# Expert weights of a routed FFN in one 8 MB and two 2 MB transfers instead of eight smaller ones

## The chip, the core and the metric

The kernel runs on one core of a Trainium2 chip. A core has TensorE (PE; its weight loads are PEld), VectorE (DVE), ScalarE (ACT), GpSimd (POOL) and SyncE (SP), which issues almost all transfers here, and 16 DMA engines that move the bytes. The metric is the device time of one execution in microseconds, as a median of runs. MB in this text is 2^20 bytes, except in the GB/s and MB columns of the profile.

## What is computed

A decoder layer on 256 tokens of width 1024: RMSNorm, a combined projection, three token mixers (attention, short convolution, cross-attention), a gated merge and an output projection, and after it a mixture of 32 experts of which each token takes four. In fp32, an expert's up matrix is 1024 x 2048 (8 MB) and its down matrix 1024 x 1024 (4 MB):

```python
def expert_block(args):
    xb, e = args
    gu = xb @ w_gu[e] + b_gu[e]
    g = jnp.minimum(gu[:, :D_EXPERT], SWIGLU_LIMIT)
    lin = jnp.clip(gu[:, D_EXPERT:], -SWIGLU_LIMIT, SWIGLU_LIMIT)
    glu = g * jax.nn.sigmoid(SWIGLU_ALPHA * g)
    return ((lin + 1.0) * glu) @ w_down[e] + b_down[e]
```

Each token's four results are weighted and added to the residual stream, and a last RMSNorm follows. All 32 experts are used, so 384 MB of expert weights have to come out of HBM whatever the routing.

## The kernel before

Raw instruction streams, one per engine, tied together by semaphores. The first 300 us compute the mixers; the rest is a loop over the 32 experts, each with 64 token slots (a second pass over the experts would run only if an expert drew more than 64 tokens).

**Buffers.** `ring` has 16 slots of 8 KB per partition. Up matrices go in as 8 slots each: even experts in slots 8 to 15, odd experts in 0 to 7, so two ups fit. `dring` has four such slots and holds one down matrix. PE counts what it has used up: `pieces_used` goes up by one for each of an expert's eight up slots, `downs_used` by one for each of its four down slots.

**Transfers.** SP issues them all in one order and waits before each for the slots that it overwrites. `expert_up` issues four transfers of 2 MB (`up_pair`: 256 rows of the matrix, two neighbouring rows and so a run of 16 KB for each partition). `expert_down` issues four of 1 MB (`down_piece`: 256 rows, two rows and so 8 KB for each partition). Each lands on its own semaphore (`piece_in`, `down_in`), and PE waits for each just before the matmuls that read it. Which row lies on which partition doesn't matter to the sum, as long as the moving operand is permuted alike: ACT writes `h2` and DVE writes the hidden product in that permuted order.

**Order on SP.** Experts 0 and 1's ups and expert 0's down are loaded while the mixers still run. After that comes the main loop: up(2), down(1), up(3), down(2), and so on up to up(23), down(22): a down comes one expert behind the ups. Then down(23), and the last eight experts in order: up(24), down(24), ..., up(31), down(31). I call the second part the in-order stretch and the place between them, where down(22) and down(23) follow each other directly, the switch. `b_down` and the last norm's gain come behind down(31).

**Order on PE.** For each expert: up matmuls (L1256, 64 recorded matmuls), then what lies between (transposes, the gather of the next tokens, the scatter of the expert before; ACT and DVE make the hidden product), then down matmuls (L1292, 32), and on to the next expert. Expert by expert, in order.

Of the kernel before, what the change touches and what calls it, by code (L numbers as in the profile page):

```python
# [18 lines left out]
P = 128  # L19
# [6 lines left out]
E = 32  # L26
# [88 lines left out]
def build(nc, a, out, scratch, ctx):  # L115
# [110 lines left out]
    in_pairs = "p (j q c) -> p j c q"  # L226
    hid_pairs = hid.rearrange(in_pairs, j=2, c=2)
    sg_pairs = sg.rearrange(in_pairs, j=2, c=2)
    hid_even_odd = g_sb.rearrange("p (j c q) -> p j c q", j=2, c=2)
# [8 lines left out]
    g_pairs = region_r[:, 6140:6148]  # L238
# [16 lines left out]
    def sem(name):  # L255
        return ctx.enter_context(nc.semaphore(name))
# [6 lines left out]
    final_gain_in, out_done, g_pairs_in = sem("final_gain_in"), sem("out_done"), sem("g_pairs_in")  # L263
# [38 lines left out]
    def _(sp):  # L302
# [34 lines left out]
        def up_pair(expert, slot, m):  # L337
            sp.dma_start(ring[:, slot:slot + 2, :].rearrange("p k n -> p (k n)"),  # L338
                         a["w_gu"][0, bass.ds(expert, 1), m * 256:(m + 1) * 256, :]
                         .rearrange("e (p k) n -> p (e k n)", k=2)).then_inc(piece_in[slot], 16)  # L340

        def expert_up(expert, slot0, uses):
# [5 lines left out]
        def down_piece(expert, j):  # L348
            sp.dma_start(dring[:, j, :], a["w_down"][0, bass.ds(expert, 1), j * 256:(j + 1) * 256, :]
                         .rearrange("e (p c) n -> p (e c n)", c=2)).then_inc(down_in[j], 16)  # L350

        def expert_down(expert, uses):
# [7 lines left out]
        for n in range(MIX_RING):  # L360
            used = N_MIX - MIX_RING + 1 + n
            sp.wait_ge(pieces_used, used)
            if n < MIX_RING - 8 and n % 2:
                up_pair(0, 8 + n - 1, n // 2)
            elif n % 2:
                up_pair(1, n - (MIX_RING - 8) - 1, (n - (MIX_RING - 8)) // 2)
            if used == N_PROJ + 12:
                down_piece(0, 2)
            if used == N_PROJ + 17:
                down_piece(0, 0)  # L370
                down_piece(0, 1)
            if used == N_MIX - 1:
                up_pair(0, 14, 3)
            if used == N_MIX:
                up_pair(0, 12, 2)
        down_piece(0, 3)
# [27 lines left out]
    def _(pool):  # L404
# [14 lines left out]
        pool.dma_start(g_pairs.rearrange("p (m k) -> p m k", k=2),  # L419
                       bass.AP(a["rows"].tensor, 16 * P, [[2, P], [256, 4], [1, 2]])).then_inc(g_pairs_in, 16)  # L420
# [3 lines left out]
    def _(act):  # L424
# [180 lines left out]
    def _(dve):  # L605
# [288 lines left out]
        def gathered_half(ps, n, half):  # L894

            dve.tensor_tensor(xg[n][:, 4 * half:4 * half + 4, :], ps[:, :].rearrange("p (c s) -> p c s", c=4),  # L896
                              g_pairs[:, 4 * half:4 * half + 4].unsqueeze(2).broadcast_to([P, 4, 2 * SLOTS]), ALU.mult)\
                .then_inc(xg_sb, 1)
# [35 lines left out]
        dve.wait_ge(g_pairs_in, 16)  # L934
# [8 lines left out]
        with dve.Fori(0, more * (E // 4) + E // 4) as i:  # L943
            for u in range(4):
# [12 lines left out]
                dve.tensor_tensor(hid_even_odd, hid_pairs, sg_pairs, ALU.mult).then_inc(hid_ready, 1)  # L957
# [32 lines left out]
    def _(pe):  # L990
# [251 lines left out]
        with pe.Fori(0, more * (E // 4) + E // 4) as i:  # L1242
            for u in range(4):
                s = i * 4 + u
                slot0 = 8 if u % 2 == 0 else 0

                pe.wait_ge(up_read, s + 1)
# [38 lines left out]
                for c in range(KC):  # L1286
                    if c % 2 == 0:
                        pe.wait_ge(down_in[c // 2], (s + 1) * 16)
                    lhsT = hidT[:, (c % 4) * P + 64 * (c // 4):(c % 4) * P + 64 * (c // 4) + 64]
# [4 lines left out]
                    if c % 2:  # L1294
                        last.then_inc(downs_used, 1)

# [44 lines left out]
```

## Time and profile before

| | |
|---|---|
| median of 3 runs | 1223.33 us (1222.9 to 1224.2) |
| span of the profiled execution | 1221.0 us |
| PE busy | 1116.0 us (91%) |
| DVE, ACT busy | 387.3 us (32%), 263.7 us (22%) |
| moved by DMA | 452.06 MB, mean 370 GB/s |

The span is that of one profiled execution; it is 2.3 us short of the median, which has what lies around it. The page cuts the span into 40 slices of 30.5 us. Landing is when a transfer's semaphore reaches its full count, and is read from SP's issue rows.

### The profile page before, as it was taken

How to read it: one execution, taken by the hardware profiler on the slowest of the kernel's cores; microseconds unless marked ns; L12 is line 12 of the kernel's file. 1: busy time of each engine (PE TensorE's matmuls, PEld its weight loads, DVE VectorE, ACT ScalarE, POOL GpSimd, SP SyncE). 2: the span in 40 equal slices, each digit the busy share in tenths (PEclk: the TensorE clock that was granted, in tenths of full speed). 3: DMA queues.
4: the chain of work that ended last, by engine and by line, in shares of the span. 5: the costliest groups of instructions: out<-in, count | busy, mean ns of one | idle time of the engine just before them, and what ended most of it. 6: DMA issues, size and time to landing. Idle time of an engine off the chain costs nothing.

```text
span 1221.0 us, 15367 instructions
## 1 busy us (share of the span) xinstructions
PE 1116.0 (91%) x6083; PEld 581.7 (48%) x6083; DVE 387.3 (32%) x716; ACT 263.7 (22%) x403; POOL 9.0 (1%) x11
## 2 busy tenths in 40 slices
PE   5999999998999988888888898898888899988886
PEld 4999999995343333333333333333333333333332
DVE  6657655574122212212121212122222222221213
ACT  5334475443011111111111111111111111111112
POOL 2000000000000000000000000000000000000000
PEclk8999999999999999999999999999999999999998
DMA  7984354667999999999999999999999999999994
GB/s 263 346 271 158 120 165 161 235 234 309 428 425 425 426 428 426 426 427 427 426 427 426 427 426 426 427 427 426 425 426 425 428 426 425 428 426 425 428 424 189
DMA packets 74642, 452.06 MB, mean 370 GB/s; under 512 B 5058, under 2 KB 36023, under 8 KB 41847
## 3 DMA queue, kind: packets, MB, share of 16 engines
q1 hardware_dynamic: 74055, 449.94, 90.3%
q0 software_dynamic: 560, 1.74, 0.5%
q8 instruction: 20, 0.33, 0.1%
q14 instruction: 7, 0.06, 0.0%
HBM read 450.60 MB, written 1.06 MB: 370 GB/s over the span
## 4 chain that ended last, share of the span: by engine, by line
DMA 50%; PE 43%; DVE 4%; SPq 1%; issue 1%; ACT 0%; DVEq 0%; ACTq 0%
DMA dring<-in_w_down_dram 40%; PE bank L1001 19%; PE bank L1256 10%; DMA ring<-in_w_gu_dram 9%; PE bank L1292 9%; SPq L338 1%; DVE region_r L954 1%; DVE region_r L957 1%; DVE region_r L950 1%; PE bank L1276 1%; DVE region_r L951 1%; PE bank L1226 1%; PE bank L1178 1%; DVE memT_low L645 0%; PE bank L1065 0%
## 5 line engine op out<-in xcount | busy, mean ns | idle before, releaser
L1256 PE MATMUL bank<-ring,region_x 128*64 128x512 f32 x2048 | 449.6, 595 | 14.4 <-DMA ring<-in_w_gu_dram 14.4
L1292 PE MATMUL bank<-dring,region_r 128*64 128x512 f32 x1024 | 241.2, 608 | 55.3 <-DMA dring<-in_w_down_dram 54.4
L1256 PEld LDWEIGHTS bank<-ring,region_x 128*64 128x64 f32 x2048 | 143.0, 137 | 300.6 <-issue 273.6
L1292 PEld LDWEIGHTS bank<-dring,region_r 128*64 128x64 f32 x1024 | 67.9, 138 | 214.4 <-DMA dring<-in_w_down_dram 109.1
L950 DVE TENSOR_SCALAR region_r<-bank 128x512 f32<-128x512 f32 x32 | 22.1, 692 | 371.3 <-PE bank L1256 371.3
L968 DVE SCALAR_TENSOR_TENSOR y_parts<-bank,region_r,y_parts 64x512 fp32r<-64x512 f32 x32 | 23.8, 744 | 338.1 <-ACT y_parts L589 338.1
L580 ACT ACTIVATE region_r<-region_r 128x512 f32<-128x512 f32 x32 | 20.1, 629 | 436.3 <-DVE region_r L950 436.3
L1001 PE MATMUL bank<-hT_high,w_high 128*128 128x256 f32 x384 | 111.0, 289 | 0.0
L1001 PE MATMUL bank<-hT_low,w_high 128*128 128x256 f32 x384 | 108.8, 283 | 0.0
L1001 PE MATMUL bank<-hT_high,w_low 128*128 128x256 f32 x384 | 108.8, 283 | 0.0
L655 DVE TENSOR_TENSOR w_low<-ring,w_high 128x2048 fp32r<-128x2048 f32 x39 | 89.2, 2290 | 55.4 <-ACT w_high L443 55.1
L443 ACT ACTIVATE w_high<-ring 128x2048 fp32r<-128x2048 f32 x40 | 76.4, 1911 | 73.2 <-PE bank L1001 71.2
L588 ACT ACTIVATE y_parts<-bank,region_r 64x512 fp32r<-64x512 f32 x32 | 21.8, 682 | 300.1 <-PE bank L1292 300.1
L1001 PEld LDWEIGHTS bank<-hT_high,w_high 128*128 128x128 f32 x384 | 73.7, 192 | 2.0 <-issue 1.7
L1001 PEld LDWEIGHTS bank<-hT_low,w_high 128*128 128x128 f32 x384 | 73.7, 192 | 0.5 <-issue 0.5
L1001 PEld LDWEIGHTS bank<-hT_high,w_low 128*128 128x128 f32 x384 | 73.7, 192 | 0.0
L1220 PE MATMUL bank<-region_r,region_h 128*128 128x128 f32 x544 | 66.2, 276 | 1.4 <-DVE region_r L890 1.4
L1220 PEld LDWEIGHTS bank<-region_r,region_h 128*128 128x128 f32 x544 | 63.4, 192 | 1.5 <-issue 1.5
L1178 PE MATMUL bank<-y_parts,scaT 128*128 128x512 f32 x132 | 47.6, 444 | 0.0
L585 ACT ACTIVATE region_r<-bank 128x512 f32<-128x512 f32 x32 | 19.1, 598 | 55.0 <-PE bank L1276 55.0
L1226 PE MATMUL bank<-b_parts,sel 128*128 128x512 f32 x65 | 29.2, 449 | 1.3 <-DVE region_x L896 0.7
L1276 PE MATMUL bank<-consts,region_r 128*128 128x128 f32 x128 | 21.0, 287 | 9.6 <-DVE region_r L957 9.6
(230 smaller groups left out, 909.1 us busy)
## 6 DMA issues: line engine op xcount, KB each, us to landing
ring<-in_w_gu_dram SPq DMA_DIRECT2D x128, 2048.0 KB, 29.6
dring<-in_w_down_dram SPq DMA_DIRECT2D x128, 1024.0 KB, 27.2
ring<-in_w_in_dram SPq DMA_DIRECT2D x26, 1024.0 KB, 9.6
ring<-in_w_mem_kv_dram SPq DMA_DIRECT2D x4, 1024.0 KB, 11.7
ring<-in_w_out_dram SPq DMA_DIRECT2D x4, 1024.0 KB, 4.8
ring<-in_w_br_conv_dram SPq DMA_DIRECT2D x2, 1024.0 KB, 5.0
ring<-in_w_br_att_dram SPq DMA_DIRECT2D x2, 1024.0 KB, 6.1
ring<-in_w_br_xatt_dram SPq DMA_DIRECT2D x2, 1024.0 KB, 5.2
```

What stands on the lines that cost most here:

```text
L443: act.activation(w_high[p % 3][:, :], ring[:, q, :], ACT.Copy).then_inc(w_high_ready, 1)
L588: act.activation(y_parts[0:64, 0:512], y_ps[0:64, :], ACT.Copy, scale=w_slot[0:64, :])
L655: dve.tensor_tensor(w_low[q][:, :], ring[:, q, :], w_high[p % 3][:, :].bitcast(fp32), ALU.subtract)\
L950: dve.tensor_scalar(g_sb, gate_ps[:, :], LIMIT, None, ALU.min).then_inc(g_ready, 1)
L968: dve.scalar_tensor_tensor(y_parts[64:128, 0:512], y_ps[0:64, :], w_slot[0:64, :], y_parts[0:64, 0:512].bitcast(fp32), ALU.mult, ALU.subtract)
L1001: ins = mm(dst, lhsT[l][at_l], rhs[r][at_r], start=first and n == 0, stop=last and n == 2)
L1178: last = mm(acc[t][half][:, :], scaT[n][:, t, :], y_parts[:, half * 512:half * 512 + 512], start=False, stop=stop)
L1220: last = mm(ps[:, c * P:(c + 1) * P], h2[:, t, at:at + P], gat[:, t, :], start=(t == 0), stop=(t == TT - 1))
L1226: mm((gate_ps, lin_ps)[k][:, :], sel[:, :], b_parts[:, k * 512:k * 512 + 512], start=True, stop=False)
L1256: last = mm(ps[64 * half:64 * half + 64, :], xg[u // 2][:, c, 64 * (u % 2):64 * (u % 2) + 64], ring[:, slot0 + c, k * F + half * 512:k * F ...
L1276: last = transpose(gate_ps[:, c * P:(c + 1) * P], g_sb[:, c * P:(c + 1) * P], ident)
L1292: last = mm(y_ps[64 * half:64 * half + 64, :], lhsT, dring[:, c // 2, at:at + 512], start=(c == 0), stop=(c == KC - 1))
```

## The change

The up matrix of an expert is loaded by one transfer of 8 MB: partition p gets rows 8p to 8p+7, one run of 64 KB. The down matrix comes in two transfers of 2 MB, four rows of each half for a partition, one run of 16 KB. So SP waits for all eight up slots to be free before it issues an up, and for two down slots before each half of a down; PE waits for a whole up before its first up matmul, and for half a down. The bytes, the buffers and the order of matrices on SP stay as they were.

At the edges the transfers keep their former sizes: experts 0 and 1's ups, expert 0's down, up(2) (four of 2 MB) and up(31) (four of 2 MB) and down(31) (four of 1 MB). There a run is cut from the 64 KB (or 16 KB) row group, so it is again 16 KB (8 KB) long. PE's loop over four experts becomes a function, called in the loop for experts 0 to 27 and once more, written out, for 28 to 31, because only there it waits for the smaller transfers again. The permutations on ACT and DVE follow the new row order.

```diff
+        def up_chunks(expert, slot, c, n):
+            sp.dma_start(ring[:, slot:slot + n, :].rearrange("p k n -> p (k n)"),
+                         a["w_gu"][0, bass.ds(expert, 1), :, :]
+                         .rearrange("e (p k) n -> p (e k n)", k=KC)[:, c * PIECE:(c + n) * PIECE]).then_inc(piece_in[slot], 16)
-            for m in range(KC // 2):
-                sp.wait_ge(pieces_used, uses + 2 * m + 1)
-                up_pair(expert, slot0 + 2 * m, m)
+        def expert_up(expert, slot0, uses, n=KC):
+            for c in range(0, KC, n):
+                sp.wait_ge(pieces_used, uses + c + n - 1)
+                up_chunks(expert, slot0 + c, c, n)
-            for j in range(DRING):
-                sp.wait_ge(downs_used, uses + j)
-                down_piece(expert, j)
+        def expert_down(expert, uses, n=2):
+            for j in range(0, DRING, n):
+                sp.wait_ge(downs_used, uses + j + n - 1)
+                down_slots(expert, j, n)
...
+        expert_up(2, 8, N_MIX - RING + 17, 2)
+        expert_down(1, 1)
+        expert_up(3, 0, N_MIX - RING + 25)
+        expert_down(2, 5)
-        with sp.Fori(0, more * (E // 2) + (E // 2 - 1 - IN_ORDER)) as i:
+        with sp.Fori(1, more * (E // 2) + (E // 2 - 1 - IN_ORDER)) as i:
...
-        with sp.Fori(0, IN_ORDER) as i:
+        with sp.Fori(0, IN_ORDER - 1) as i:
...
+        expert_up(E - 2, 8, ups + (E - 2) * KC)
+        expert_down(E - 2, downs + (E - 2) * DRING)
+        expert_up(E - 1, 0, ups + (E - 1) * KC, 2)
+        expert_down(E - 1, downs + (E - 1) * DRING, 1)
...
-            act.activation(h2[:, t, :].rearrange("p (m k q) -> p m k q", m=4, k=2),
-                           x2[:, t, :].rearrange("p (m q k) -> p m k q", m=4, k=2),
+            act.activation(h2[:, t, :].rearrange("p (k q) -> p k q", k=8),
+                           x2[:, t, :].rearrange("p (q k) -> p k q", k=8),
...
-                dve.tensor_tensor(hid_even_odd, hid_pairs, sg_pairs, ALU.mult).then_inc(hid_ready, 1)
+                dve.tensor_tensor(hid_by_row, hid_fours, sg_eights, ALU.mult).then_inc(hid_ready, 1)
...
-                    if c % 2 == 0:
+                    if c == 0:
                         pe.wait_ge(piece_in[slot0 + c], i * 32 + 16 * (u // 2) + 16 * (loads_before(slot0 + c) + 1))
+                    elif c % 2 == 0 and (u < 3 or last_one):
+                        pe.wait_ge(piece_in[slot0 + c], 16 * (loads_before(slot0 + c) + 1 + u // 2))
...
-                    if c % 2 == 0:
+                    if c % 4 == 0:
                         pe.wait_ge(down_in[c // 2], (s + 1) * 16)
+                    elif c % 2 == 0:
+                        pe.wait_ge(down_in[c // 2], 32 if last_one else 16)
```

On SP at the start of the expert loop: `ring` transfers are ups, `dring` transfers downs, 128x4096 is 16 KB for each partition. Before, one half of the loop body, which loads one up and one down:

```order
L338 ISA [waits pieces_used]
L338 DMA ring<-in_w_gu_dram 128x4096
L345 REGISTER_ALU
L338 ISA [waits pieces_used]
L338 DMA ring<-in_w_gu_dram 128x4096
L345 REGISTER_ALU
L338 ISA [waits pieces_used]
L338 DMA ring<-in_w_gu_dram 128x4096
L345 REGISTER_ALU
L338 ISA [waits pieces_used]
L338 DMA ring<-in_w_gu_dram 128x4096
```

Now, what stands ahead of the loop, for up(2), down(1), up(3) and down(2):

```order
L339 DMA ring<-in_w_gu_dram 128x4096 [waits pieces_used] x4
L352 DMA dring<-in_w_down_dram 128x4096 [waits downs_used] x2
L339 DMA ring<-in_w_gu_dram 128x16384 [waits pieces_used]
L352 DMA dring<-in_w_down_dram 128x4096 [waits downs_used] x2
```

Up(3) is the first that has one wait, for the last of its eight slots, in the place of four.

On SP at the switch, down(23) behind down(22). Before:

```order
L349 DMA dring<-in_w_down_dram 128x2048 [waits downs_used]
L355 REGISTER_ALU
L349 DMA dring<-in_w_down_dram 128x2048 [waits downs_used]
L355 REGISTER_ALU
L349 DMA dring<-in_w_down_dram 128x2048 [waits downs_used]
L355 REGISTER_ALU
L349 DMA dring<-in_w_down_dram 128x2048 [waits downs_used]
L388 UNCONDITIONAL_BRANCH
```

Now:

```order
L352 DMA dring<-in_w_down_dram 128x4096 [waits downs_used]
L359 REGISTER_ALU
L352 DMA dring<-in_w_down_dram 128x4096 [waits downs_used]
L396 UNCONDITIONAL_BRANCH
```

The first half of down(23) waits until PE has used two slots of down(22), where its first quarter waited for one.

## Rows read from the trace of the kernel before

**Rows 1.** The page: DMA share and rate in 40 slices, packets, chain by engine.

```profile
DMA  7984354667999999999999999999999999999994
GB/s 263 346 271 158 120 165 161 235 234 309 428 425 425 426 428 426 426 427 427 426 427 426 427 426 426 427 427 426 425 426 425 428 426 425 428 426 425 428 424 189
DMA packets 74642, 452.06 MB, mean 370 GB/s; under 512 B 5058, under 2 KB 36023, under 8 KB 41847
DMA 50%; PE 43%; DVE 4%; SPq 1%; issue 1%; ACT 0%; DVEq 0%; ACTq 0%
```

**Rows 2.** Waits in total: engine, line, what for; us, times, longest.

```profile
PE bank L1292 <- DMA dring<-in_w_down_dram: 54.4, 68, 1.6
```

**Rows 3.** Timeline of PE: start, length; down(s) as its quarters land, 600-660 us.

```profile
624.00 1.94 PE L1292 MATMUL bank<-dring,region_r 128*64 128x512 f32 x8 [1.53 <-DMA dring<-in_w_down_dram]
...
631.46 1.94 PE L1292 MATMUL bank<-dring,region_r 128*64 128x512 f32 x8 [0.55 <-DMA dring<-in_w_down_dram]
```

**Rows 4.** The same, the last up and what follows, 1180-1211 us.

```profile
1182.44 3.65 PE L1256 MATMUL bank<-ring,region_x 128*64 128x512 f32 x16 [0.62 <-DMA ring<-in_w_gu_dram]
...
1192.22 3.65 PE L1256 MATMUL bank<-ring,region_x 128*64 128x512 f32 x16 [1.24 <-DMA ring<-in_w_gu_dram]
...
1200.22 7.09 PE L1292 MATMUL bank<-dring,region_r 128*64 128x512 f32 x32
1207.23 3.70 PE L1300 MATMUL bank<-ring,region_r 32*128 32x512 f32 x8
```

**Rows 5.** Windows: stretch, engines' busy us, PEclk, DMA share, GB/s; mixer weights load.

```profile
40.00:45.00 5.00, 5.00 (x44) 5.00 (x43) 2.98 (x2) 1.92 (x1) 0.00 (x0) 1.00 1.10 348
```

**Rows 6.** Timeline of SP: the four issues of up(3).

```profile
328.25 10.58 SPq L338 DMA_DIRECT2D ring<-in_w_gu_dram  x4
```

**Rows 7.** One issue by line: the first of up(2), with its time to landing.

```profile
L338 SPq DMA_DIRECT2D ring<-in_w_gu_dram x1: 346/346/346, 302.6 to 302.6; - x1
...
DMA to landing us min/median/max: 7.7/7.7/7.7
```

**Rows 8.** The same, the last of up(3).

```profile
L338 SPq DMA_DIRECT2D ring<-in_w_gu_dram x1: 332/332/332, 338.5 to 338.5; - x1
...
DMA to landing us min/median/max: 17.1/17.1/17.1
```

**Rows 9.** Timeline of PE: up(1), down(1), up(2), 320-352 us.

```profile
324.38 13.96 PE L1256 MATMUL bank<-ring,region_x 128*64 128x512 f32 x64
...
342.68 7.09 PE L1292 MATMUL bank<-dring,region_r 128*64 128x512 f32 x32
...
350.12 13.96 PE L1256 MATMUL bank<-ring,region_x 128*64 128x512 f32 x64
```

**Rows 10.** Timelines at the switch: PE at down(22), SP at down(23).

```profile
948.68 1.94 PE L1292 MATMUL bank<-dring,region_r 128*64 128x512 f32 x8 [1.54 <-DMA dring<-in_w_down_dram]
...
956.12 1.94 PE L1292 MATMUL bank<-dring,region_r 128*64 128x512 f32 x8 [0.54 <-DMA dring<-in_w_down_dram]
...
950.66 7.77 SPq L349 DMA_DIRECT2D dring<-in_w_down_dram  x4
```

**Rows 11.** Windows and PE's timeline at 800 us; then the window at 15 us.

```profile
800.00:805.00 5.00, 3.92 (x12) 1.12 (x14) 0.00 (x0) 0.00 (x0) 0.00 (x0) 0.66 1.02 423
...
801.08 7.07 PE L1292 MATMUL bank<-dring,region_r 128*64 128x512 f32 x24 [1.51 <-DMA dring<-in_w_down_dram]
...
15.00:20.00 5.00, 0.38 (x1) 0.38 (x2) 4.67 (x6) 2.03 (x6) 2.84 (x2) 0.63 1.10 348
```

**Rows 12.** The page, section 6: a 1 MB transfer with runs of 4 KB.

```profile
ring<-in_w_out_dram SPq DMA_DIRECT2D x4, 1024.0 KB, 4.8
```

**Rows 13.** By line: DVE's contiguous product, its permuted one, ACT's h2; min/median/max ns.

```profile
L954 DVE SCALAR_TENSOR_TENSOR region_r<-region_r x32: 691/693/694, 314.0 to 1197.3; 128x512 f32<-128x512 f32 x32
...
L957 DVE TENSOR_TENSOR region_r<-region_r x32: 691/691/695, 314.8 to 1198.0; 128x512 f32<-128x512 f32 x32
...
L568 ACT ACTIVATE region_h<-region_x,norm 128x1024 f32<-128x1024 f32 x2 | 2.3, 1202 | 0.0
```

More of the change, by code:

```diff
@@ L225, in build @@
     hidT = region_r[:, 3072:3584]
[L226 to L229, printed above, removed]
+    in_fours = "p (q k) -> p k q"
+    hid_fours = hid.rearrange(in_fours, k=4)
+    sg_eights = sg.rearrange(in_fours, k=4)
+    hid_by_row = g_sb.rearrange("p (k q) -> p k q", k=4)
     x2T = region_r[:, 0:2048].rearrange("p (c t) -> p c t", c=KC)
@@ L335, in _, with down_slots @@
         sp.dma_start(x_again, a["x"][0].rearrange("(t p) d -> p t d", p=P)).then_inc(x_again_in, 16)
[L337 to L342, printed above, removed]
-            for m in range(KC // 2):
-                sp.wait_ge(pieces_used, uses + 2 * m + 1)
-                up_pair(expert, slot0 + 2 * m, m)
[L348 to L352, printed above, removed]
-            for j in range(DRING):
-                sp.wait_ge(downs_used, uses + j)
-                down_piece(expert, j)
+        def up_chunks(expert, slot, c, n):
[6 more added lines that the diff above has]
+                up_chunks(expert, slot0 + c, c, n)
+        def down_slots(expert, j, n):
+            m, k = j // 2, j % 2
+            sp.dma_start(dring[:, j:j + n, :].rearrange("p k n -> p (k n)"),
+                         a["w_down"][0, bass.ds(expert, 1), m * 512:(m + 1) * 512, :]
+                         .rearrange("e (p k) n -> p (e k n)", k=4)[:, k * PIECE:(k + n) * PIECE]).then_inc(down_in[j], 16)
+        def expert_down(expert, uses, n=2):
+            for j in range(0, DRING, n):
+                sp.wait_ge(downs_used, uses + j + n - 1)
+                down_slots(expert, j, n)
         for n in range(MIX_RING):
@@ L363, in _ @@
             if n < MIX_RING - 8 and n % 2:
-                up_pair(0, 8 + n - 1, n // 2)
+                up_chunks(0, 8 + n - 1, n - 1, 2)
             elif n % 2:
-                up_pair(1, n - (MIX_RING - 8) - 1, (n - (MIX_RING - 8)) // 2)
+                up_chunks(1, n - (MIX_RING - 8) - 1, n - (MIX_RING - 8) - 1, 2)
             if used == N_PROJ + 12:
-                down_piece(0, 2)
+                down_slots(0, 2, 1)
             if used == N_PROJ + 17:
-                down_piece(0, 0)
-                down_piece(0, 1)
+                down_slots(0, 0, 1)
+                down_slots(0, 1, 1)
             if used == N_MIX - 1:
-                up_pair(0, 14, 3)
+                up_chunks(0, 14, 6, 2)
             if used == N_MIX:
-                up_pair(0, 12, 2)
-        down_piece(0, 3)
+                up_chunks(0, 12, 4, 2)
+        down_slots(0, 3, 1)
         sp.wait_ge(passes_ready, 1)
         more = sp.value_load(more_i32[0:1, 0:1], min_val=0, max_val=PASSES - 1)
-        with sp.Fori(0, more * (E // 2) + (E // 2 - 1 - IN_ORDER)) as i:
+        expert_up(2, 8, N_MIX - RING + 17, 2)
[3 more added lines that the diff above has]
+        with sp.Fori(1, more * (E // 2) + (E // 2 - 1 - IN_ORDER)) as i:
             expert_up((i * 2 + 2) % E, 8, i * 16 + (N_MIX - RING + 17))
@@ L418, in _ @@
         pool.dma_start(b_rt, a["b_router"].broadcast_to([P, E])).then_inc(router_in, 16)
-        pool.dma_start(g_pairs.rearrange("p (m k) -> p m k", k=2),
-                       bass.AP(a["rows"].tensor, 16 * P, [[2, P], [256, 4], [1, 2]])).then_inc(g_pairs_in, 16)
+        pool.dma_start(g_eights, bass.AP(a["rows"].tensor, 16 * P, [[8, P], [1, 8]])).then_inc(g_eights_in, 16)
     @block.scalar
@@ L896, in gathered_half @@
             dve.tensor_tensor(xg[n][:, 4 * half:4 * half + 4, :], ps[:, :].rearrange("p (c s) -> p c s", c=4),
-                              g_pairs[:, 4 * half:4 * half + 4].unsqueeze(2).broadcast_to([P, 4, 2 * SLOTS]), ALU.mult)\
+                              g_eights[:, 4 * half:4 * half + 4].unsqueeze(2).broadcast_to([P, 4, 2 * SLOTS]), ALU.mult)\
                 .then_inc(xg_sb, 1)
@@ L933, in _ @@
         bias_selector(0)
-        dve.wait_ge(g_pairs_in, 16)
+        dve.wait_ge(g_eights_in, 16)
         dve.wait_ge(gathered, 1)
@@ L1241, in _, with four_experts @@
         more = pe.value_load(more_i32[0:1, 0:1], min_val=0, max_val=PASSES - 1)
-        with pe.Fori(0, more * (E // 4) + E // 4) as i:
+        def four_experts(i, last_four):
             for u in range(4):
@@ L1245, in _ @@
                 slot0 = 8 if u % 2 == 0 else 0
+                last_one = last_four and u == 3
                 pe.wait_ge(up_read, s + 1)
@@ L1295, in _ @@
                         last.then_inc(downs_used, 1)
+        with pe.Fori(0, more * (E // 4) + (E // 4 - 1)) as i:
+            four_experts(i, False)
+        four_experts(more * (E // 4) + (E // 4 - 1), True)
         pe.wait_ge(b_down_in, 16)
```

4 lines of the change are left out of this document (2 added, 2 removed).

## The prediction

> **What bounds the kernel now.** I read the page's slices first. From slice 11 to slice 39, some 880 of 1221 us, the DMA engines are busy all the time and move 424 to 428 GB/s [rows 1]; the chain puts half of the span on DMA. Then the waits: PE stands 54 us in total ahead of its down matmuls until a quarter of a down lands, in 68 waits of at most 1.6 us [rows 2]. An expert takes PE 25.74 us from the start of one up to the start of the next when nothing is late (350.12 - 324.38) [rows 9]. The transfers take longer. Quarters of a down land 2.487 us apart (7.46/3) [rows 3], quarters of an up 4.89 us (9.78/2) [rows 4], so an expert takes the engines 4 x 4.89 + 4 x 2.487 = 29.5 us. From about 305 to 1201 us the time is thus set by bytes, and only a faster stream, or a hole in it, moves the end; behind the last transfer PE counts.
>
> **What a transfer costs beyond its bytes.** Let x be the time of a MB and y what eight runs add on an engine (128 partitions on 16 engines). The page counts 32,795 packets of 8 KB or more [rows 1]; 128 ups of four and 128 downs' quarters with 128 runs each give 2 x 16,384 = 32,768, so a run is a packet. x + y = 2.487 and 2x + y = 4.89 give y = 0.084. A third point: the mixers' weights come in runs of 1 KB, 64 for each engine and MB, at 348 GB/s [rows 5], 3.01 us for a MB: x + 8y = 3.01, and with the first equation y = 0.075, x = 2.41. I take 0.075, since its lever is longer. It is a cost of the packet (9 ns), as eight times more packets in one transfer cost eight times more.
>
> The Trainium skill (DMA: Bandwidth & Descriptors, "Why small descriptors are slow") names about 3 cycles for each packet inside the engine; at the 850 MHz of its specifications that would be an estimated 28 ns for eight, and the saving below 4 us where I get 10.8. The rows show over twice that, and the measurement decides.
>
> **Saved in the stream.** Ups 3 to 30 go from four transfers to one, and 32 runs on an engine to 8: 28 x 3 = 84 times y. Downs 1 to 30 go from four to two: 30 x 2 = 60. Together 144 x 0.075 = **10.8 us** (7 to 13 by the spread of y). That the 64 KB run is still one packet isn't in the trace; see the rivals. An expert then takes 8x + y + 2(2x + y) = 19.36 + 9.79 = 29.15 us.
>
> **Added at the start.** Up(3) was issued in four parts from 328.25 on [rows 6], the last at 338.5, and that one landed at 355.6 [rows 8]. Now the whole waits for what the last part waited for, PE's end of up(1) [rows 9], so it is issued at 338.5. What was issued before it, up to down(1), would be through by 335. So the queue runs empty. Into an empty queue a 2 MB transfer landed 7.7 us after its issue [rows 7], 2.8 more than its 4.9 in the stream. Up(3) lands at 338.5 + 2.8 + 19.36 = 360.7, 5.1 later than before, though 5y = 0.4 of the saving lie ahead of that point: the hole costs **5.5 us**. From up(4) on PE frees an up well ahead. In the main loop, with L the landing of a down's second half: PE needs 3.5 for that half, 0.4 to the next up and 14 for it, so the next up is issued at about L + 18.3 and wanted at L + 29, less 2.8. That is covered.
>
> **Added at the switch.** Down(22) and down(23) follow each other in one ring. Before, PE began a quarter at 948.68 and SP refilled it at 950.66 [rows 10], 2.0 later, while 7.4 us of quarters were still in the queue. Now, with X the landing of down(22)'s second half, PE begins the first at X - 4.9 and needs 3.5 + 0.2; the refill is issued at X - 1.1 and lands at X - 1.1 + 2.8 + 4.9 = X + 6.6 where the stream would have X + 4.9: **1.7 us**. It is nothing if the 2.8 are hidden, 3.4 if PE's clock is low there.
>
> **In the in-order stretch** PE starts an up when all of it has landed, at U. It reaches down at U + 18.3 (342.68 - 324.38), frees its first half at U + 22.1, and down(e+1) may be issued from there; it is wanted at U + 29.15 less 2.8, so 4.3 us are left. PE then waits 29.15 - 25.74 = 3.4 us for each up in one piece. Before, it worked on an up while that came in, in waits of 0.62 and 1.24 us [rows 4].
>
> **Added at the end.** Before, PE started the last quarter of up(31) on its landing at 1192.22 and was done with down(31) at 1207.23, 15.0 later [rows 4]. Now PE starts up(30) at U, up(31) at U + 25.7, down(31) at U + 44.0 and is done at U + 51.05, as it can't catch up: all of up(31) is there by U + 9.79 + 4 x 4.895 = U + 29.4. That is 21.7 behind the last up's landing where it was 15.0, **6.7 us** more. Smaller pieces for expert 31 alone don't help, since PE is still busy with expert 30.
>
> **The clock.** After 1.51 us of waiting ahead of down the granted clock was 0.66 in the window 800 to 805 us, between the levels of 1.2 and 2.4 GHz, and 24 matmuls took 7.07 us [rows 11], where 32 take 7.09: 7.07 - 5.32 = 1.75 us lost. In the window 15 to 20 us, in which PE was busy for only 0.38 us, it was 0.63. The new waits of 3.4 us are over twice as long as the 1.51, so I take a fall at every up of the in-order stretch. Six of them are covered (27.5 < 29.15), that of up(30) isn't: **1.7 us** (0 to 1.7).
>
> The Trainium skill (TensorE: Matmul & The Clock Gate, "HAM oscillation") says that waiting for a transfer ahead of each group of matmuls makes each group start slow. By it the 1.7 are due; without it the sum is 1.7 less.
>
> **Nothing, or bounded.** DVE's permuted product (step 2) takes 691 ns, the contiguous one 693 [rows 13], so a step of 4 should cost nothing; were it doubled, 0.7 us an expert would disappear in PE's waits, save one or two at the end. ACT's h2 reads with step 8 where it was 2, 1.2 us each [rows 13]: 0, at most 2.3 once. The runs of the edge transfers are as long as before. PE's written-out last four experts might have to be fetched behind long packets; the slack of the in-order stretch covers a few us.
>
> A longer run may land later: runs of 4 KB landed 4.8 us after issue [rows 12], about 2.2 more than their 2.6 in the stream, runs of 16 KB 2.8 more. Drawn on in proportion to 64 KB this adds 2.4 once at the start and once at the end. I take 0, being nearest to the row of 16 KB, and keep 4.8 for the range.
>
> **Sum** against the profiled span of 1221.0: -10.8 + 5.5 + 1.7 + 6.7 + 1.7 = +4.8, so 1225.8; with the 2.3 us between span and median, 1228.1. The three edges eat the saving and more.
>
> **Rivals.**
> 1. *Edges cheaper, within 0.2%.* No fall of the clock at up(30), and the refill at the switch hidden: +1.4, 1224.7. For it: behind the wait of 1.54 us at 948.68 [rows 10] the eight matmuls took 1.94 us, as they do at full clock.
> 2. *Faster.* Long runs also raise the rate of bytes. About 350 MB are in the new transfers; each 1% off x = 2.41 is worth 8.4 us, so 1219.7 at 1%. It decides from 0.9% on, where 7.2 us more are saved and the sum passes -2.4. Against it: runs of 1, 8 and 16 KB fit one x, so nothing points to a better one. The Trainium skill (DMA: Bandwidth & Descriptors, "Specifications") gives the port side a ceiling of 435 GB/s, which is this x; by it the rival can't be.
> 3. *The 64 KB run is cut*, into four of 16 KB as before: the ups' 84y = 6.3 are lost, +11.1, 1234.4. The trace has no run over 16 KB.
> 4. *Long runs disturb each other in HBM.* Runs of neighbouring partitions start 64 KB apart where it was 16, so what is read at once lies four times further apart. At 1% it costs 8.4 us: 1236.5. No row here speaks for or against it. The Trainium skill (DMA: Bandwidth & Descriptors, "Latency and other measured facts") tells of row pitches of 2 MB and more that cut the rate and one of 512 KB that didn't; 64 KB is below them.
> 5. *Late landing of long runs*, above: +9.6, 1232.9.
>
> **Chances.** Forecast 0.47; rival 1 0.22; 2 0.13; 3 0.08; 4 0.05; 5 0.05. A measurement of this kernel can tell about 0.2% (2.4 us) from no change, so: faster 0.13, same 0.22, slower 0.65. The range 1221 to 1236 leaves out the better half of rival 2 and the worse of 4.
>
> **What would show it.** In the trace after: a DMA slice near 340 us with a hole of 5 us; landings of an expert 29.15 us apart (29.5: rival 3; under 29.0: rival 2; over 29.6: rival 4); packets near 74,600 - 84 x 128 - 60 x 128 = 56,200 (67,000 if cut); PE waits of 3.4 us ahead of ups in the last 230 us with a clock under 1.00 behind them; PE's end of down(31) 21.7 to 23.4 us behind the last up's landing. Without the hole or the longer end the forecast is wrong.

## The result, and the profile after

The changed kernel takes **1235.7 us** (median of 4 runs, 1231.1 to 1236.8) where the kernel before takes 1223.7 beside it: 1.009 times as long, 95% interval 1.0077 to 1.0102, so 0.9% slower. The forecast was 1228.1 us with a range of 1221 to 1236: the direction is right, the time lies 0.3 us inside the upper edge of the range, and the loss is 12 us where I had 4.8. The profiled execution is the shortest of the four, with a span of 1229.1 us, 8.1 over that of before.

The page after: share and rate in 40 slices, packets, chain. To be read beside [rows 1].

```profile
DMA  7984344667899999999999999999999999999992
GB/s 260 344 274 162 120 168 146 240 252 303 374 387 439 433 444 420 433 444 416 437 444 414 439 444 414 427 430 433 431 431 432 394 429 417 429 432 430 431 424 93
DMA packets 53910, 452.13 MB, mean 368 GB/s; under 512 B 2754, under 2 KB 33719, under 8 KB 39543
DMA 50%; PE 44%; DVE 3%; ACT 1%; issue 1%; SPq 0%; DVEq 0%; ACTq 0%
```

The stream is faster in the middle (432 GB/s on average from 500 to 900 us, where it was 426), and three places are worse: slices 11 and 12 (374 and 387), slice 32 (394), and the last, which holds almost no transfers any more (93 where it was 189). There are 14,367 packets of 8 KB or more; 32,795 - 84 x 128 - 60 x 128 = 14,363 were due if a run of 64 KB is one packet. So rival 3 is out by the row of packets. 2,304 packets under 512 B are gone too. That is 144 transfers fewer times 16 engines, so each transfer brings a small packet on each engine; experiment 2, with three transfers more, has 49 more of them.

**The start.** Windows (engines' busy us, PEclk, DMA share, GB/s), then the one issue of up(3) with its landing, in the changed kernel:

```profile
335.00:337.00 2.00, 2.00 (x12) 0.72 (x10) 0.00 (x0) 0.00 (x0) 0.00 (x0) 1.00 0.02 8
337.00:339.00 2.00, 2.00 (x13) 0.58 (x8) 0.00 (x0) 0.00 (x0) 0.00 (x0) 1.00 0.00 0
...
L339 SPq DMA_DIRECT2D ring<-in_w_gu_dram x1: 328/328/328, 339.6 to 339.6; - x1
...
DMA to landing us min/median/max: 23.2/23.2/23.2
```

Here is the hole: 4 us in which nothing moves, while PE is busy. Up(3) is issued at 339.6 and lands at 362.8, where its last part landed at 355.6 [rows 8].

**The main loop and the switch.** PE's timeline at down(22), and SP's issues of down(23) and up(24):

```profile
950.61 3.65 PE L1309 MATMUL bank<-dring,region_r 128*64 128x512 f32 x16 [1.63 <-DMA dring<-in_w_down_dram]
955.48 3.65 PE L1309 MATMUL bank<-dring,region_r 128*64 128x512 f32 x16 [1.21 <-DMA dring<-in_w_down_dram]
...
988.22 15.65 PE L1271 MATMUL bank<-ring,region_x 128*64 128x512 f32 x64 [2.53 <-DMA ring<-in_w_gu_dram]
...
954.31 5.20 SPq L352 DMA_DIRECT2D dring<-in_w_down_dram  x2
960.06 0.35 SPq L339 DMA_DIRECT2D ring<-in_w_gu_dram  x1
```

Each matmul group that waits starts on a landing. From down(22)'s second half to the whole of up(24) it takes 988.22 - 955.48 = 32.7 us; a down and an up in the stream are 29.15. The bubble, a stretch in which the queue has too little to do, is 3.6 us. It comes in two equal parts: the refill issued at 954.31 lands at 962.15, 6.7 us behind down(22), and the one issued at 959.17 lands at 968.83, 6.7 us behind the first, where 4.9 were due each time.

**The end.** PE's timeline from up(30) on. Compare [rows 4]:

```profile
1134.87 15.65 PE L1271 MATMUL bank<-ring,region_x 128*64 128x512 f32 x64 [2.04 <-DMA ring<-in_w_gu_dram]
...
1164.03 13.95 PE L1271 MATMUL bank<-ring,region_x 128*64 128x512 f32 x64 [1.27 <-DMA ring<-in_w_gu_dram]
...
1182.70 7.09 PE L1309 MATMUL bank<-dring,region_r 128*64 128x512 f32 x32
1190.14 13.95 PE L1271 MATMUL bank<-ring,region_x 128*64 128x512 f32 x64
...
1208.82 7.09 PE L1309 MATMUL bank<-dring,region_r 128*64 128x512 f32 x32
1215.84 3.70 PE L1321 MATMUL bank<-ring,region_r 32*128 32x512 f32 x8
```

From up(30)'s landing on PE never waits for a transfer again; up(31) starts 26.1 us later, though three of its four parts had landed. The last part lands at 1193.4, PE is done with down(31) 22.4 us after that, where it took 15.0.

**Two costs that I had put at nothing.** By line: DVE's product and PE's wait for it, ACT's h2 and PE's gather behind it.

```profile
L968 DVE TENSOR_TENSOR region_r<-region_r x32: 1057/1069/1082, 315.6 to 1206.3; 128x512 f32<-128x512 f32 x32
...
  PE bank L1291: 21.7, 32
...
289.06 4.17 ACT L579 ACTIVATE region_h<-region_x,norm 128x1024 f32<-128x1024 f32 x2
...
293.28 3.84 PE L1231 MATMUL bank<-region_r,region_h 128*128 128x128 f32 x32 [2.07 <-ACT region_h L579]
```

DVE's product takes 1069 ns with a step of 4 elements where it took 691 with a step of 2 [rows 13], and PE waits 0.68 us for it in each expert where it waited 0.30. ACT's two h2 instructions take 4.17 us together where they took 2.31, and PE now stands 2.07 us before the gather and begins it 0.85 us later.

Where the 8.1 us of this execution are, by the same events in both traces (positive: later than before):

| event | before | after | step |
|---|---|---|---|
| PE starts up(1) | 324.38 | 325.62 | +1.2: h2, product |
| up(3) has landed | 355.6 | 362.8 | +6.0: hole |
| down(22) has landed | 956.1 | 955.5 | -7.8: 102 times eight packets less |
| down(23) has landed | 966.0 | 968.9 | +3.5: switch |
| up(31) has landed | 1192.2 | 1193.4 | -1.7: 35 times eight packets less (2.7), 1.0 lost again, 0.8 of it at up(29) |
| PE is done with down(31) | 1207.2 | 1215.8 | +7.4: end |

That is +8.6, and what follows is 0.5 shorter. Up to down(22) the 102 are 20 ups (4 to 23) at 3 and 21 downs (2 to 22) at 2, so eight packets cost 7.8/102 = 0.076 us, which I had read as 0.075. The two steps at the hole and the switch are net of such savings, 0.4 and 0.15.

### The profile page after: what moved, and what is told of

Read it like the earlier page. It is cut to its first block, busy times and chain, and to the rows that moved or that the text cites. A ratio compares the mean times of both kernels' runs of the same rounds, so it can differ in the third digit from the quotient of the medians.

```text
span 1229.1 us, 14723 instructions
## 1 busy us (share of the span) xinstructions
PE 1117.4 (91%) x6083; PEld 588.3 (48%) x6083; DVE 399.1 (32%) x716; ACT 266.1 (22%) x403; POOL 8.8 (1%) x11
## 4 chain that ended last, share of the span: by engine, by line
DMA 50%; PE 44%; DVE 3%; ACT 1%; issue 1%; SPq 0%; DVEq 0%; ACTq 0%
DMA dring<-in_w_down_dram 40%; PE bank L1012 19%; PE bank L1309 11%; DMA ring<-in_w_gu_dram 10%; PE bank L1271 9%; DVE region_r L968 1%; PE bank L1019 0%; DVE region_r L965 0%; DVE region_r L961 0%; DMA consts<-in_consts_dram 0%; DVE memT_low L656 0%; PE bank L1076 0%; PE bank L1291 0%; PE bank L1056 0%; DVE region_r L962 0%
## 5 line engine op out<-in xcount | busy, mean ns | idle before, releaser
L1271 PEld LDWEIGHTS bank<-ring,region_x 128*64 128x64 f32 x2048 | 145.7, 138 | 302.1 <-issue 285.5
L1309 PEld LDWEIGHTS bank<-dring,region_r 128*64 128x64 f32 x1024 | 72.4, 141 | 201.5 <-issue 129.1
L1231 PEld LDWEIGHTS bank<-region_r,region_h 128*128 128x128 f32 x544 | 63.3, 192 | 2.2 <-ACT region_h L579 2.2
L968 DVE TENSOR_TENSOR region_r<-region_r 128x512 f32<-128x512 f32 x32 | 34.2, 1069 | 1.1
L596 ACT ACTIVATE region_r<-bank 128x512 f32<-128x512 f32 x32 | 19.2, 599 | 66.9 <-PE bank L1291 66.9
```

Source lines behind the costliest of these rows:

```text
L968: dve.tensor_tensor(hid_by_row, hid_fours, sg_eights, ALU.mult).then_inc(hid_ready, 1)
L1231: last = mm(ps[:, c * P:(c + 1) * P], h2[:, t, at:at + P], gat[:, t, :], start=(t == 0), stop=(t == TT - 1))
L1271: last = mm(ps[64 * half:64 * half + 64, :], xg[u // 2][:, c, 64 * (u % 2):64 * (u % 2) + 64], ring[:, slot0 + c, k * F + half * 512:k * F ...
L1309: last = mm(y_ps[64 * half:64 * half + 64, :], lhsT, dring[:, c // 2, at:at + 512], start=(c == 0), stop=(c == KC - 1))
```

## Experiments

Times are medians; "changed" is the changed kernel. All are beside runs of the kernel before on the same chip (1223.8 to 1224.2 us).

**1. The changed kernel again**, for what its longer executions have more.

> The changed kernel once more, for a second trace of it: its four executions so far lay between 1231.1 and 1236.8 us and the trace in hand is that of the shortest. My account of that trace against before (span 1229.1 against 1221.0): -10.4 us in the stream, +1.2 from a longer h2 on ACT, +6.0 hole at up(3), +3.6 at the switch, +7.4 at the end, +1 of scatter. I expect this trace to show the same terms within 1 us, plus what the longer executions have more, 3 to 5 us: either a fall of TensorE's clock at up(30) (1.7 us, up matmuls 15.65 instead of 13.95 us), or, if the rival is right that long runs make the 16 engines run apart, landings late by several us somewhere in the stream with a longer hole behind them.

Measured: 1233.7 us (1231.8 to 1235.8), the trace's span 1233.8, 4.7 over the first trace. The stream is the same: ups are issued 29.14 us apart ((917.63 - 480.56)/15) as in the first ((915.42 - 478.36)/15). The difference stands in two rows of PE, each with its window:

```profile
294.13 5.47 PE L1231 MATMUL bank<-region_r,region_h 128*128 128x128 f32 x32 [2.07 <-ACT region_h L579]
...
294.00:299.00 5.00, 4.87 (x29) 4.87 (x30) 3.12 (x18) 0.07 (x1) 0.00 (x0) 0.66 0.75 320
...
1165.73 16.87 PE L1271 MATMUL bank<-ring,region_x 128*64 128x512 f32 x64 [2.95 <-DMA ring<-in_w_gu_dram]
...
1165.00:1172.00 7.00, 6.26 (x16) 1.86 (x18) 1.13 (x5) 0.07 (x1) 0.00 (x0) 0.53 0.99 421
```

Behind the wait for h2 the granted clock is 0.66 and the gather takes 5.47 us where it took 3.84: 1.6. Behind the wait for up(30) it is 0.53, nearly all of those 7 us at the lower level of 1.2 GHz, and the up takes 16.87 us where it takes 13.95: 2.9, with nothing behind it to cover them. The first trace had neither fall. Of the start's 2.5 us (1.6, and 0.9 of a mixer stage that ended later) 1.7 are left when up(30) lands (1165.73 against 1164.03), and 1.7 + 2.9 is the 4.7. So between these two traces the difference is for the most part TensorE's clock behind new waits, and the engines running apart were not needed to explain it.

All the traces taken together show how far this goes. Eight of them have the wait of 2.07 us for h2: five then take 5.3 to 5.5 us for the gather and three take 3.84. Seven load up(30) whole: it takes 13.95 us in the first trace alone, 15.65 in three, and 16.87 to 16.96 in three. The first trace is the exception, and its wait there was the shortest (1.27). Up(30) in experiments 2 and 4:

```profile
1162.86 15.65 PE L1271 MATMUL bank<-ring,region_x 128*64 128x512 f32 x64 [2.94 <-DMA ring<-in_w_gu_dram]
...
1163.39 16.96 PE L1271 MATMUL bank<-ring,region_x 128*64 128x512 f32 x64 [3.13 <-DMA ring<-in_w_gu_dram]
```

**2. Up(3) in four transfers.**

```diff
-        expert_up(3, 0, N_MIX - RING + 25)
+        expert_up(3, 0, N_MIX - RING + 25, 2)
```

> Up(3) in four transfers of 2 MB again, all else as in the changed kernel. Theory (the queue runs empty because up(3) waits for all eight slots): landing of up(3)'s last part 6 us earlier, no hole near 340 us, time 5.5 to 6 us under the changed kernel. Rival (the hole is made good later, since PE is the bound in the first experts and waits there anyway): within 1 us of the changed kernel.

Measured: 1231.3 us (1229.5 to 1233.7), 2.4 under the first experiment, with ranges that overlap, so neither. The landing of up(3) did come 7.1 us earlier, counted from expert 0's start (341.7 + 16.1 - 301.6 = 56.2, where changed has 63.3). But the next up has the hole. Its window and issue:

```profile
362.00:370.00 8.00, 8.00 (x47) 3.98 (x44) 2.03 (x4) 1.11 (x3) 0.00 (x0) 1.00 0.82 315
...
L339 SPq DMA_DIRECT2D ring<-in_w_gu_dram x1: 352/352/352, 368.0 to 368.0; - x1
...
DMA to landing us min/median/max: 23.2/23.2/23.2
```

Again 23.2 us from issue to landing, the time of a whole up into an empty queue. Down(2) was through at 357.8 + 9.8 = 367.6, and up(4) would have landed at 387.0; it landed at 391.2, 4.2 later. PE gains 3 us an expert on the stream (26.1 against 29.15), so a whole up can be issued without a hole only when PE has caught up by that much. The hole was real, and mending one up returns what the next then doesn't lose: 7.1 - 4.2 = 2.9, of which the median shows 2.4.

**3. Up(30) in four transfers.**

```diff
-        expert_up(E - 2, 8, ups + (E - 2) * KC)
+        expert_up(E - 2, 8, ups + (E - 2) * KC, 2)
```

> Up(30) in four transfers of 2 MB, all else as in the changed kernel. Theory (PE starts up(30) only when all of it is there and can't catch up in the last two experts): PE's end of down(31) goes from 22.4 us behind the last up's landing to about 15.3, time 7 us less, save 0.2 for three more times the cost of eight packets. Rival (the end is set by the landing of down(31) and the tail behind it): at most 2 us less.

Measured: 1229.7 us (1229.0 to 1230.9), 4.0 under the first experiment, of which the missing wait and fall of the clock at up(30) is a part. The expectation of 7 failed. The timeline:

```profile
1137.03 13.95 PE L1271 MATMUL bank<-ring,region_x 128*64 128x512 f32 x64 [1.41 <-DMA ring<-in_w_gu_dram]
1155.71 7.09 PE L1309 MATMUL bank<-dring,region_r 128*64 128x512 f32 x32
1163.15 13.95 PE L1271 MATMUL bank<-ring,region_x 128*64 128x512 f32 x64
...
1214.95 3.70 PE L1321 MATMUL bank<-ring,region_r 32*128 32x512 f32 x8
```

The last up in one piece is now up(29), and from its landing at 1137.03 PE needs three chains of 26.1 without a wait: 77.9 us. The last part of up(31) is due 2 x (9.79 + 19.58) = 58.7 after up(29), so PE ends 19.2 behind it, not 15.3. It is the same step that made 22.4 with one small up: each further one gives back only 29.4 - 26.1 = 3.3 us, and it takes three or four to come back to 15.

**4. Downs in four transfers of 1 MB.**

```diff
-        def expert_down(expert, uses, n=2):
+        def expert_down(expert, uses, n=1):
```

> Every down in four transfers of 1 MB with runs of 8 KB, ups as in the changed kernel. Theory (a cost of 9.4 ns for each packet, and a bubble at the switch because half a down has to be free before the refill): +60 x 0.078 = +4.7 us in the stream, -3.6 at the switch, together +1.1; expert period 29.30 where the changed kernel has 29.14; the chain after down goes from 3.5 to 1.8 us behind the last landing, which hides nothing. Rival (no bubble at the switch, its late landing is skew between engines that would come anyway): +4.7.

Measured: 1235.7 us (1233.5 to 1236.9), span 1231.5. The period is (916.12 - 476.81)/15 = 29.29 us, as the cost for each packet wants. At the switch:

```profile
958.25 1.94 PE L1307 MATMUL bank<-dring,region_r 128*64 128x512 f32 x8 [0.55 <-DMA dring<-in_w_down_dram]
960.54 13.95 PE L1271 MATMUL bank<-ring,region_x 128*64 128x512 f32 x64
...
987.53 12.67 PE L1271 MATMUL bank<-ring,region_x 128*64 128x512 f32 x58 [0.81 <-DMA ring<-in_w_gu_dram]
```

987.53 - 958.25 = 29.3, which is a down in quarters (9.93) and a whole up (19.36) without a bubble. So the bubble is made by handing over the down in halves. The times, 0 to 2 over changed, fit the +1.1 better than the +4.7, but the spread is as large; the period and the row above decide, not the medians.

**5. One transfer, short runs.** The changed kernel's transfers, with the rows laid out as before.

```diff
+                sp.dma_start(ring[:, slot:slot + n, :].rearrange("p (m k) n -> p m (k n)", k=2),
+                             a["w_gu"][0, bass.ds(expert, 1), :, :]
+                             .rearrange("e (m p k) n -> p (e m) (k n)", k=2, p=P)).then_inc(piece_in[slot], 16)
```

> The changed kernel's transfers, waits and edges (ups of 8 MB, downs of two times 2 MB), but with the rows on the partitions as before: an up is one transfer of four runs of 16 KB for each partition, half a down one of two runs of 8 KB. The permutations on ACT and DVE are those of before again. Theory (the stream's saving is a cost of 9.4 ns for each packet): expert period back at 29.5 us where the changed kernel has 29.14, and h2 and DVE's product back at 1.2 and 0.69 us each; +10.4 for the stream, -1.2 to -2.8 for the start (no clock fall at the gather), -0.8 at the end: about 1241. Rival (it is a cost of the transfer): period stays at 29.15, time about 1231.

Measured: 1240.2 us (1238.0 to 1241.5), 1.0129 times before (1.0112 to 1.0145). The period is (921.43 - 478.64)/15 = 29.52 us, that of before. An 8 MB transfer of 16 KB runs is as slow as four of 2 MB: what the stream gains hangs on the packets and not at all on the number of transfers. This kernel has all the coarse waits and none of the gain, and shows their price alone, with the falls of the clock that they bring: 1.3%.

**6. The rows alone.** Transfers and waits as before, rows and permutations as in the changed kernel.

```diff
-        def expert_up(expert, slot0, uses, n=KC):
+        def expert_up(expert, slot0, uses, n=2):
-        def expert_down(expert, uses, n=2):
+        def expert_down(expert, uses, n=1):
```

> The changed kernel's rows on the partitions and its permutations on ACT and DVE, with the transfers and waits of before: ups in four of 2 MB (16 KB runs, now 64 KB apart in HBM), downs in four of 1 MB (8 KB runs, 16 KB apart). Theory (the permutation costs by ACT's h2, 4.2 us where it was 2.3, and by DVE's product, 1.07 where it was 0.69; the pitch of the runs costs nothing): period 29.5, start +1.2, with a fall of the clock at the gather +2.8, end +0.4: 1.6 to 3.2 us over before, and hardly any longer waits of PE for a transfer in the last experts. Rival (runs further apart slow the stream): period above 29.6.

Measured: 1225.5 us (median of 10, 1224.7 to 1225.9), 1.0010 times before (1.0001 to 1.0020), so 1.3 us more (0.1 to 2.4). Period (903.78 - 490.49)/14 = 29.52. So the step of 64 KB between runs costs the stream nothing, and the permutations cost about 1.3 us. That is a little below the expected 1.6 to 3.2; its trace had no fall of the clock at the gather (3.84 us). In it down(22) lands 0.5 us later than before, and PE is done with down(31) 1.0 later.

**7. Walking the other way.** The changed kernel, product and h2 with contiguous reads and strided writes.

```diff
-    hid_by_row = g_sb.rearrange("p (k q) -> p k q", k=4)
+    hid_by_row = g_sb.rearrange("p (k q) -> p q k", k=4)
```

> The changed kernel with DVE's product and ACT's h2 walked in the order of their inputs: contiguous reads and strided writes where the changed kernel reads strided and writes contiguous. For their durations: theory (a strided read of 16 bytes or more is what costs) 0.69 us for the product and 1.2 for h2; rival (the stride costs on either side) 1.07 and 2.1 or more.

```profile
L968 DVE TENSOR_TENSOR region_r<-region_r x32: 1037/1046/1049, 317.5 to 1211.7; 128x512 f32<-128x512 f32 x32
...
L579 ACT ACTIVATE region_h<-region_x,norm x2: 2002/2026/2049, 289.7 to 291.5; 128x1024 f32<-128x1024 f32 x2
```

1046 and 2026 ns: the stride costs on either side, and the rival was right (nearly so for h2, where it had 2.1 or more). (One run, 1236.7 us.)

**8. Edges mended.** Ups 3 to 5 and 28 to 31 in four, down(23) in four, the middle as in the changed kernel. PE's groups with such waits are written out.

```diff
+        expert_up(3, 0, N_MIX - RING + 25, 2)
+        expert_up(4, 8, 16 + N_MIX - RING + 17, 2)
+        expert_up(5, 0, 16 + N_MIX - RING + 25, 2)
...
+        expert_down(e0 - 1, downs + DRING * (e0 - 1), 1)
...
+        expert_up(E - 4, 8, ups + (E - 4) * KC, 2)
+        expert_up(E - 3, 0, ups + (E - 3) * KC, 2)
+        expert_up(E - 2, 8, ups + (E - 2) * KC, 2)
```

> The changed kernel with its edges mended: ups 3, 4 and 5 and ups 28 to 31 in four transfers of 2 MB, down(23) in four of 1 MB, all else in one and two transfers. After the second experiment the hole only moved on to up(4), so three ups are given back at the start; after the third PE is the bound from the last whole up's landing, 26.1 us an expert, so four at the end. Theory: stream saves 22 x 3 + 59 x 2 - 2 = 124... taken as 66 + 58 = 124 times 0.078 = 9.7 us against before; left are +1.2 (with a clock fall +2.8) for h2 and +0.4 at the end: 1215 to 1217, faster than before by 7 us. Rival (whole transfers in the middle leave other losses, such as waits for the whole of an up in the four experts 24 to 27 with falls of the clock): above 1219.

Measured: 1221.2 us (median of 10, 1218.5 to 1222.6), 0.9976 times before (0.9966 to 0.9986): faster by 0.24%, and 12 to 14 us under changed. The mechanism holds, the size is 4 short of the expectation. PE's last rows:

```profile
1190.89 3.65 PE L1278 MATMUL bank<-ring,region_x 128*64 128x512 f32 x16 [1.25 <-DMA ring<-in_w_gu_dram]
1199.26 7.09 PE L1316 MATMUL bank<-dring,region_r 128*64 128x512 f32 x32
1206.27 3.69 PE L1333 MATMUL bank<-ring,region_r 32*128 32x512 f32 x8
```

15.4 behind the last landing: the long end is gone. Up(6), the first whole one, landed 29.1 us after up(5), so the hole is gone too. Its trace shows what is missing: expert 0 starts at 301.39, 2.8 later than before (h2, with a fall of the clock), an up landing 1.3 us late at 563 us and the third part of another 1.2 late at 1156.6, for which I have no cause, and at the switch 983.55 - 952.31 = 31.2 us where 29.3 were due, as the refill in quarters follows a down that still lands in halves.

**9. TensorE reads with a step** in the place of the permutations, else as changed.

```diff
-                    last = mm(ps[:, c * P:(c + 1) * P], h2[:, t, at:at + P], gat[:, t, :],
+                    row = h2[:, t, :].rearrange("p (q k) -> p k q", k=8)[:, 4 * half + c, :]
+                    last = mm(ps[:, c * P:(c + 1) * P], row, gat[:, t, :],
```

> The changed kernel, but the new row order is no longer made by ACT and DVE: h2 and the hidden product are written contiguous in their natural order, and TensorE reads its stationary operand with a step of 8 (gather) or 4 elements (transposes of the hidden product). Theory (of the loss, 1.2 us are h2's 1.9 longer on ACT, 1.6 in some executions the fall of TensorE's clock behind that wait, 0.4 per expert DVE's product): h2 back to 1.2 us, the product to 0.69, expert 0's first up matmul at or before 298.6 us in all executions, chain of an expert 25.74 us, end 0.8 us shorter; 2 to 3.6 us under the changed kernel, about 1231. Rival (the stride then costs on TensorE): weight loads of the gather over 192 ns, chain at or over 26.1, no gain.

```profile
L1230 PEld LDWEIGHTS bank<-region_r,region_h x544: 312/335/340, 292.6 to 1218.8; 128*128 128x128 f32 x182
...
L1290 PEld LDWEIGHTS bank<-consts,region_r x128: 196/206/212, 322.8 to 1219.8; 128*128 128x128 f32 x128
...
292.58 7.89 PE L1230 MATMUL bank<-region_r,region_h 128*128 128x128 f32 x32 [1.41 <-DVE region_r L900]
```

Measured: 1243.5 us (1239.9 to 1243.9), 8 to 10 worse than changed; the rival was right. The gather's weight loads take 335 ns with a step of 8 where they take 192, and the gather of an expert 3.97 us where it took 1.95. The chain of an expert is 27.3 us (331.84 to 359.12). It lengthens the end twice over, by experts 30 and 31, and delays every issue of a whole up at the start. The transposes' loads, with a step of 4, take 206 ns where they took 140. H2 did go back to 2.17 us for both and the product to 0.69, but the gather ahead of expert 0 takes 7.89 us where it took 3.84, and expert 0's up matmuls take 15.65 (granted clock 0.76 from 302.8 to 310 us). So up(1) starts at 331.84, 6.2 us later than in the changed kernel, which is half of what this span has over the first trace's (1241.8 against 1229.1).

**10. Experiments 8 and 9 together.**

> Both together: edges mended as in the eighth experiment, and TensorE reading with a step in the place of the permutations. Theory: 2 to 3.5 us under the eighth (1221.2), so 1218, faster than before by 5 to 6 us (0.5%). Rival (the losses at the start are swallowed by PE's slack in the first experts): no less than the eighth.

Measured: 1229.5 us (1226.8 to 1232.5), 8 worse than experiment 8. The same cause (the first gather takes 7.89 us here too), and again the edges are worth 14 us.

**11. Experiment 8, with the step on TensorE only in the four transposes**; ACT permutes h2, DVE writes the product as it comes.

```diff
-                dve.tensor_tensor(hid_by_row, hid_fours, sg_eights, ALU.mult).then_inc(hid_ready, 1)
+                dve.tensor_tensor(g_sb, hid, sg, ALU.mult).then_inc(hid_ready, 1)
-                    last = transpose(gate_ps[:, c * P:(c + 1) * P], g_sb[:, c * P:(c + 1) * P], ident)
+                    last = transpose(gate_ps[:, c * P:(c + 1) * P], g_sb.rearrange("p (q k) -> p k q", k=4)[:, c, :], ident)
```

> The eighth experiment's kernel, with h2 permuted by ACT as in the changed kernel (its strided reading on TensorE cost 2 us an expert), but the hidden product written in its natural order by DVE and read with a step of 4 elements by TensorE's four transposes, whose weight loads took 206 ns each in that form where they took 140: four times 0.07 = 0.3, hidden or not, against DVE's 0.38 us. Theory: chain of an expert 25.8 to 26.1 us, up to 0.3 less than in the eighth; 0 to 1 us under its 1221.2. Rival: no difference, as both costs lie in the same place of the chain.

Measured: **1219.1 us** (1218.5 to 1220.5), 0.9958 times before (0.9944 to 0.9971): faster by 0.42%, the best of all here. It is 2.1 us under experiment 8, more than the 0 to 1 expected. The chain is back at 25.75 us (301.07 to 326.82), so the product's cost is gone. Between the two traces (spans 1219.6 and 1218.5) the shorter chain shows as 0.3 us at the end, and the late landing of 1156.6 is missing here, worth 1.2. How much of the 2.1 between the medians is the product's, one trace each doesn't tell.

## Why the prediction was right, and where it was off

That the time came out inside the range is in part luck. The range went on to 1236 so as to take in rivals 3 and 5 and the milder half of 4, and of these only 1.0 us of rival 5 came true. What filled the room were terms that I had too small or at nothing.

**The stream** (-10.8): right in mechanism and size. The cost is that of a packet, experiment 5 shows it, and it measured 0.076 us for eight, so 10.9 for the 144; 7.8 of them are seen between up(3) and down(22). The Trainium skill (DMA: Bandwidth & Descriptors, "Why small descriptors are slow") has an overhead of about 3 cycles for each, from which I estimated 28 ns for eight and so 4 us for the 144. The runs show 76 ns and contradict it for this stream. A run of 64 KB is one packet. Rivals 2, 3 and 4 are out: an expert takes 29.14 us, forecast 29.15.

**The hole at the start** (+5.5): measured 6.0 in the table, and 6.4 as my term counts it, without the 0.4 saved ahead of it. Landing came 23.2 us after issue where 22.2 were reckoned: the longer run lands 1.0 us later, so rival 5 is a small truth (1.0, not 2.4). My sentence that from up(4) on PE is well ahead was true only because up(3) was late. (The parts that I gave there for the main loop add up to 17.9, not to 18.3; nothing hangs on it.)

**The switch** (+1.7, up to 3.4): measured 3.5 to 3.6. The mechanism is right by experiment 4, the size isn't. I had reckoned the refill of the first half alone, and that one landed 7.8 us after its issue where I had 7.7, 1.8 late where I had 1.7. The second half's refill was issued at 959.2 and landed 9.7 later, which costs as much again; why these 2 us, the runs don't settle.

**The end** (+6.7): measured 7.4, 0.7 of it being DVE's longer product in two experts. The step on which the term rests, that small pieces for expert 31 alone don't help, is shown by experiments 3 and 8.

**The clock** (+1.7): here a term was mis-sized. It is not one value: in seven traces up(30) lost 0 once, 1.7 three times and 2.9 to 3.0 three times, which is over the bound of 1.7. The bound came from a wait of 1.5 us; the waits at up(30) last up to 3.7. And a second such place, the gather behind h2, wasn't in the sum at all: 1.5 to 1.6 in five traces of eight. These two are most of the difference between the two traces of the changed kernel; its other executions left none. Nor did every up of the in-order stretch bring a fall: in the first trace four of the seven whole ups from 24 to 30 took 15.65 us. A slow up shortens the next wait by 1.7, to some 1.3 us in three of these four cases, and behind those waits the next up ran at full clock. The Trainium skill's rule (TensorE: Matmul & The Clock Gate, "HAM oscillation") held in kind: new waits for transfers ahead of a group of matmuls made it start slow (15.65 or 16.9 us for an up of 13.95), though not each time.

**Put at nothing** (0, bounds 0.7 and 2.3): the step that failed. "A step of 4 should cost nothing" was drawn from a step of 2, and the product went from 691 to 1069 ns. h2 took 1.9 longer, within its bound. Together 1.2 at the start and 0.7 at the end, and they opened the wait behind which the clock falls. The Trainium skill (SBUF — State Buffer, "Door 1: The DMA port swizzle") says that SBUF has lines of 16 bytes, that full speed wants at least two hits in each, and also that 4 fp32 can be strided for free. The rows agree with the two hits (a step of 2 fp32 leaves two in a line and costs 691 ns, a step of 4 leaves one and costs 1069) and contradict the free stride of 4. That the lines are the cause is argued here, not shown: no run changed the type.

Summed with what was measured: -9.5 + 6.0 + 3.5 + 6.7 + 1.9 = +8.6 for the shortest execution. I had 4.8. The 3.8 between them are the strides (1.9), the switch (1.9), the landing of the long run (0.9 to 1.0) and what was lost behind the switch (1.0), less the fall of the clock that didn't come there (1.7) and 0.1 of stream. The second trace lost 4.5 more to the clock, of which part was regained before up(30); its span is 12.8 over that of before, where the medians say 12.

## What to carry to other kernels

In a stream that is kept full, a longer contiguous run buys some 9.5 ns of an engine's time for each packet saved; putting several runs into one transfer buys nothing. The price of a coarse transfer is not in the stream but where the stream starts, turns and ends: issue waits for the last slot, the consumer waits for the last byte, and at the end the whole chain of the last coarse piece stands behind it. Keep coarse pieces to the steady part, and make as many small ones at either edge as the consumer needs to catch up (here three ups at the start and four at the end, as PE gains some 3 us on the stream with each); and price every stride that a new layout brings to the engines by its own step, not by a shorter one.

## What I had not expected of the hardware

- DVE's product of two fp32 operands costs 691 ns for 512 elements with a step of 2 and 1069 with a step of 4 on the operands that it reads, or 1046 with the step on the one that it writes. ACT goes from 1202 ns for 1024 elements with a step of 2 to about 2.1 us with a step of 8.
- TensorE's weight loads depend on the stationary operand's step: 335 ns where they took 192 at a step of 8 elements, 206 where they took 140 at 4.
- A wait of 2.07 us by PE was followed by a fall of the clock in one execution and by none in another of the same kernel, and in five of eight traces in all; one such place makes a kernel's time spread by 1.6 us, up(30) by 2.9.
